# Norms between the stages of an eight-stage fp32 network, done one tile of 128 tokens at a time instead of for all 256 tokens at once

## The chip, the cores and the metric

One Trainium2 chip, of which this kernel uses one core. The metric is the device time of one execution in microseconds (us); lower is better. The core's engines run side by side, each through its own instruction stream: TensorE (PE, with its weight loads PEld), VectorE (DVE), ScalarE (ACT), GpSimd (POOL), and SyncE (SP), which issues most transfers. They wait for each other through semaphores.

## The reference

256 tokens of 1024 features pass through two blocks of four stages each. All is fp32.

```python
# block 1, RMSNorm BEFORE each stage; x keeps the plain sum
x = x + short_conv_mixer(rmsnorm(x, norm_mixer[0]))      # CONV
x = x + swiglu(rmsnorm(x, norm_ffn[0]))                  # FFN0, d_ff 2816
x = x + swa_sink_attention(rmsnorm(x, norm_mixer[1]))    # SWA
x = x + swiglu(rmsnorm(x, norm_ffn[1]))                  # FFN1
# block 2, LayerNorm AFTER each stage, x is replaced by it
x = layer_norm(1.414 * x + attention_mixer(x))           # NA
x = layer_norm(1.414 * x + squared_relu_mlp(x))          # MLP0, d_ff 4096
x = layer_norm(1.414 * x + mamba2_bidir_mixer(x))        # SSM
x = layer_norm(1.414 * x + squared_relu_mlp(x))          # MLP1 -> out
```

A norm needs the whole row of a token, so a token's norm can't begin before the last column of the stage ahead is summed into that token.

## The kernel before

**Chunks.** The weights come in 202 chunks of 128x2048 fp32 (1 MB), in one order for the whole kernel, through three slots. SyncE loads a chunk into `raw`; ACT rounds it to fp32r in `whi` (`hi(c)`, L828); DVE takes the rest, `raw - whi`, into `wlo` (`lo(c)`, L1185). `hi(c)` waits until TensorE is through with chunk `c - 3`. Every product is done in three matmuls: high by high, high by low, low by high. Activations are split the same way into `acthi` and `actlo`.

**Two shapes of product.** A *feature chunk* (`feature_chunk` L418; used for gate/up, MLP up, the convolution's and most of SSM's inputs) has a 128x128 block of the weights stationary and all 256 tokens of `acthi`/`actlo` moving: 8 contraction blocks x 3 x 2 feature halves = 48 matmuls of 256 columns, both token tiles in each. A *token chunk* (`token_chunk` L430; attention inputs, and the out-projections in `project` L454) has a 128-token tile stationary and 256 weight columns moving: 48 matmuls too, 24 for each tile `m`. A *down chunk* (`down_products` L487, the last one `last_down` L500 with L496) has a hidden tile stationary and 512 columns moving, 24 matmuls, 12 for each token tile. Its four results stand in the PSUM banks `ACC` to `ACC + 3`, kept open over a whole FFN or MLP by eight matmuls on zeros (`open_accumulators`, L477).

**The boundary between two stages.** There are seven boundaries where activations are made anew, called norm 1 (CONV to FFN0) to norm 7 (SSM to MLP1); norm 4 (FFN1 to NA) has no norm, only the split. The last norm, norm 8, leads to the output. At each of 1 to 7, in this order:

1. DVE adds the last pieces into `x` (L1195, or L1191 with the factor 1.414 followed by a `bn_stats`, L1193). For RMSNorm ACT squares each piece with a running sum (L836).
2. DVE sums the statistics of both tiles (L1201 or L1211); POOL makes 1/sqrt of them (`rsqrt`, L1671 and L1673); DVE scales both tiles, 128x1024 each (L1204 or L1215).
3. TensorE, which has filled its time with 24 matmuls on zeros (`keep_warm(24)`, L395), transposes 16 blocks of 128x128 into the `ACC` banks (`turn_acts`, L450).
4. ACT and DVE bring them into `acthi` and `actlo`, for norms 1 to 3 with the gain as a per-partition column (L846, L1223), for 5 to 7 after a pass with gain and bias (L856, L866, L1236, L1243). DVE also does one `lo(c)` in between. TensorE starts the first chunk two contraction blocks at a time as they come.
5. For norms 5 to 7 DVE then applies gain and bias to `x` itself, 4 passes of 128x1024 (`ln_finish`, L1252, L1254).

The stage before a boundary ends in four out-projection chunks (norms 1, 3, 5, 7) or in a last down chunk (norms 2, 4, 6, 8). Between FFN1 and NA TensorE also turns the relative position bias over (`flip_rpb`, L623: 16 matmuls of 512 columns, DVE adds the rest at L1454).

In each engine the order is that of the program text: an instruction that waits holds up all behind it on its engine.

## Time and profile before

| | |
|---|---|
| time, 3 runs | 1456.77 us median (1455.8 to 1458.49) |
| the profiled execution | 1455.31 us, of which 1453.5 us are the traced span |
| PE busy | 1359.7 us, 94% of the span |
| DVE busy | 922.3 us, 63% |
| ACT busy | 694.6 us, 48% |
| POOL busy | 210.1 us, 14% |
| TensorE's granted clock, mean | 0.96 |
| chain that ended last | PE 78%, DVE 16%, issue 2%, ACT 2% |

"Busy" of PE includes matmuls on zeros and slow ones. The granted clock is a share of 2.4 GHz: 1.00 is the upper level, 0.50 (1.2 GHz) the lower one, and a value between is a stretch with both. The busy time of a matmul in the rows is longer than the distance to the next one, since they overlap; the distance between starts is what a long series costs.

### The profile page before, as it was taken

To read this page: it belongs to the slowest core of one execution; us is meant where nothing else is said; L and a number is where in the kernel's file an instruction comes from. 1 tells how busy PE (TensorE), PEld (TensorE's weight loads), DVE (VectorE), ACT (ScalarE), POOL (GpSimd) and SP (SyncE) were. 2 spreads that over 40 slices of the span, in tenths; PEclk is the share of its full clock that TensorE was granted. 3 is DMA by queue.
4 is the path that set the end of the run, shared out by engine and by line. 5 is a ranking of instruction groups with operands and counts; after the bars stand their busy time and mean duration, and the time that the engine had idled before them with its cause. 6 is when DMAs were issued, how large, how long until landed. Compare 5 with 4: busy or idle time off the path is not lost.

```text
span 1453.5 us, 22749 instructions
## 1 busy us (share of the span) xinstructions
PE 1359.7 (94%) x9654; PEld 1274.9 (88%) x9654; DVE 922.3 (63%) x1036; ACT 694.6 (48%) x938; POOL 210.1 (14%) x227
## 2 busy tenths in 40 slices
PE   8999999998999999998999999988888878999997
PEld 8999999988899999797899999888787868899996
DVE  5655544557654454556775555787988997755555
ACT  5344444356544444335634444466656664344441
POOL 0000000016150000000000000012555665000000
PEclk9999999998799999998999999999999889999999
DMA  9554666543177656353046555544233214365552
GB/s 303 174 175 148 193 188 196 174 144 118 30 181 210 189 174 194 125 176 116 26 149 201 177 176 201 174 140 122 87 118 115 87 59 129 134 202 195 182 177 85
DMA packets 220324, 223.24 MB, mean 154 GB/s; under 512 B 7232, under 2 KB 204224, under 8 KB 220096
## 3 DMA queue, kind: packets, MB, share of 16 engines
q1 hardware_dynamic: 217472, 213.94, 46.7%
q10 hardware_dynamic: 1728, 5.76, 1.2%
q0 software_dynamic: 1024, 2.10, 0.8%
q8 instruction: 76, 1.25, 0.4%
q14 instruction: 24, 0.20, 0.0%
HBM read 220.72 MB, written 1.05 MB: 153 GB/s over the span
## 4 chain that ended last, share of the span: by engine, by line
PE 78%; DVE 16%; issue 2%; ACT 2%; POOL 1%; DMA 1%; POOLq 0%; DVEq 0%; SPq 0%; ACTq 0%
PE ps L487 19%; PE ps L402 13%; PE ps L403 13%; PE ps L404 13%; DVE ssm_taps L1544 4%; PE ps L413 4%; PE ps L415 4%; PE ps L414 4%; PE ps L749 3%; DVE wlo L1185 2%; DVE weight L1567 2%; PE ps L496 1%; PE ps L582 1%; DVE small L1374 1%; DVE weight L1573 1%
## 5 line engine op out<-in xcount | busy, mean ns | idle before, releaser
L1185 DVE TENSOR_TENSOR wlo<-raw,whi 128x2048 fp32r<-128x2048 f32 x202 | 470.3, 2329 | 228.3 <-ACT whi L828 228.3
L402 PE MATMUL ps<-acthi,whi 128*128 128x256 f32 x1664 | 477.7, 287 | 12.9 <-DVE actlo L1223 4.9
L403 PE MATMUL ps<-actlo,whi 128*128 128x256 f32 x1664 | 475.3, 286 | 0.0
L404 PE MATMUL ps<-acthi,wlo 128*128 128x256 f32 x1664 | 474.9, 285 | 0.0
L828 ACT ACTIVATE whi<-raw 128x2048 fp32r<-128x2048 f32 x202 | 385.1, 1907 | 143.5 <-PE ps L487 98.9
L402 PEld LDWEIGHTS ps<-acthi,whi 128*128 128x128 f32 x1664 | 324.1, 195 | 16.5 <-issue 11.4
L403 PEld LDWEIGHTS ps<-actlo,whi 128*128 128x128 f32 x1664 | 324.2, 195 | 2.5
L404 PEld LDWEIGHTS ps<-acthi,wlo 128*128 128x128 f32 x1664 | 323.8, 195 | 0.0
L1671 POOL TENSOR_SCALAR small<-small 128x2 f32<-128x2 f32 (+2 forms) x17 | 9.0, 528 | 1087.5 <-DVE small L1211 717.7
L487 PE MATMUL ps<-whi,hidhi 128*128 128x512 f32 x400 | 123.9, 391 | 0.0
L487 PE MATMUL ps<-wlo,hidhi 128*128 128x512 f32 x400 | 123.6, 390 | 0.0
L487 PE MATMUL ps<-whi,hidlo 128*128 128x512 f32 x400 | 123.4, 390 | 0.0
L413 PE MATMUL ps<-whi,acthi 128*128 128x256 f32 x368 | 106.7, 290 | 3.7 <-DVE actlo L1230 2.5
L414 PE MATMUL ps<-wlo,acthi 128*128 128x256 f32 x368 | 106.4, 289 | 0.0
L415 PE MATMUL ps<-whi,actlo 128*128 128x256 f32 x368 | 106.0, 288 | 0.0
L487 PEld LDWEIGHTS ps<-wlo,hidhi 128*128 128x128 f32 x400 | 75.1, 188 | 16.1
L487 PEld LDWEIGHTS ps<-whi,hidlo 128*128 128x128 f32 x400 | 75.1, 188 | 16.0
L1544 DVE SCALAR_TENSOR_TENSOR ssm_taps<-ssm_window,params,ssm_taps 128x256 f32<-128x256 f32 x128 | 73.1, 612 | 22.8 <-ACT ssm_taps L1026 21.1
L1693 POOL TENSOR_TENSOR cum<-table,ssm_small 128x512 fp32r<-128x512 f32 x64 | 74.6, 1194 | 60.0 <-PE ps L705 41.1
L902 ACT ACTIVATE gate_sb<-ps 128x256 f32<-128x256 f32 x44 | 16.9, 384 | 138.2 <-PE ps L404 138.2
L487 PEld LDWEIGHTS ps<-whi,hidhi 128*128 128x128 f32 x400 | 71.9, 189 | 11.9
L413 PEld LDWEIGHTS ps<-whi,acthi 128*128 128x128 f32 x368 | 73.1, 199 | 4.5 <-issue 4.1
(227 smaller groups left out, 1945.6 us busy)
## 6 DMA issues: line engine op xcount, KB each, us to landing
raw<-in_mlp_w SPq DMA_DIRECT2D x128, 512.0 KB, 4.3
raw<-in_ffn_w_gate_up SPq DMA_DIRECT2D x88, 512.0 KB, 5.2
raw<-in_ssm_w_in SPq DMA_DIRECT2D x50, 512.0 KB, 4.8
raw<-in_ffn_w_down SPq DMA_DIRECT2D x44, 512.0 KB, 4.3
raw<-in_conv_w_in SPq DMA_DIRECT2D x24, 512.0 KB, 5.7
raw<-in_attn_w_in SPq DMA_DIRECT2D x18, 512.0 KB, 4.5
raw<-in_ssm_w_out SPq DMA_DIRECT2D x16, 512.0 KB, 4.2
raw<-in_attn_w_qkv SPq DMA_DIRECT2D x12, 512.0 KB, 4.5
```

The lines of the kernel that those rows point to most:

```text
L402: e.matmul(out, hi[:, k, cols], acthi[:, k, :], start=k == 0 and f == 0, stop=False, skip_group_check=True)
L403: e.matmul(out, hi[:, k, cols], actlo[:, k, :], start=False, stop=False, skip_group_check=True)
L404: last = e.matmul(out, lo[:, k, cols], acthi[:, k, :], start=False, stop=k == KT - 1, skip_group_check=True)
L413: e.matmul(out, xh, hi[:, k, :], start=k == 0 and m == tokens[0], stop=False, skip_group_check=True)
L414: e.matmul(out, xh, lo[:, k, :], start=False, stop=False, skip_group_check=True)
L415: last = e.matmul(out, xl, hi[:, k, :], start=False, stop=k == KT - 1, skip_group_check=True)
L487: last = e.matmul(ps[:, ACC + 2 * m + n, :], p_, w_[:, k, n * 512:(n + 1) * 512], start=False, stop=False, skip_group_check=True)
L749: last = e.matmul(ps[:, OUT_BANKS[n], m * T:(m + 1) * T], p_, w_[:, k, :], start=half == m == k == q == 0, stop=half == 1 and k == KT - 1 ...
L828: e.activation(whi[s][:, :], raw[s][:, :], ACT.Copy).then_inc(*rounded.up(c))
L1185: e.tensor_tensor(wlo[s][:, :], raw[s][:, :], f32(whi[s][:, :]), ALU.subtract).then_inc(*split.up(c))
L1544: last = e.scalar_tensor_tensor(out=taps[:, q, f, :], in0=window[:, q, f, t:t + T], scalar=w, in1=taps[:, q, f, :], op0=ALU.mult, op1=ALU.add)
L1693: last = e.tensor_tensor(cum[d][k][:, :, :], spread(mask, [0, 4], [1, P]), spread(head_cols(v, m, d, g), [1, 4], [0, P]), ALU.mult)
```

## The change

**The tail of a stage.** The last two chunks do tile 0 first, then tile 1. Out-projection: chunk 2 tile 0, chunk 3 tile 0, chunk 2 tile 1, *transposes of tile 0*, chunk 3 tile 1. Down: both chunks' tile 0 (four groups of six matmuls), the earlier chunk's tile 1, then tile 1 of the last chunk in two halves, with the transposes of tile 0 before the first half (norms 2, 4) or between the halves (norm 6).

**The head of the next stage.** `first_feature_chunks` and `first_token_chunks` do two chunks together: chunk c tile 0, transposes of tile 1, chunk c+1 tile 0, chunk c tile 1, chunk c+1 tile 1. In a feature chunk a tile means 128 moving columns in place of 256, so its 48 matmuls become 96. At norm 6 the first chunk is the half chunk of SSM (24 matmuls, now 48).

**The norm.** It runs for a tile at a time, in halves of 512 columns. RMSNorm multiplies by scale and gain in one instruction (row gains come by a broadcast transfer into `lnrow`, also for norms 1 to 3); LayerNorm makes two such instructions a half, `(x - mean) * gain`, then `* rstd + bias`, and `x` is then final. POOL makes 1/sqrt once per tile. The split copies 128x512 at a time, two per tile. `keep_warm` at the boundaries, `open_accumulators`, `ln_finish` and the gain passes are gone. DVE's `lo` of the stage's second chunk stands between the adds and the scaling of tile 1.

**Others.** `flip_rpb` is done in two parts after the products of NA's chunks 3 and 5. The out-projection takes four PSUM banks at once: in CONV it waits for `conv_gated(3)` before its first matmul. The output leaves in four transfers in place of two.

TensorE's part first, then DVE's (`scale`, its LayerNorm branch, and `next_stage`):

```diff
-            def turn_acts(n, src, ready):
-                if n != 4:
-                    keep_warm(24)
...
+            def turn_tile(n, m):
+                src = h if n in (1, 2, 3) else x
+                for j in range(2):
+                    if n == 4:
+                        e.wait_ge(*added("ffn1", m, j))
+                    else:
+                        e.wait_ge(*scaled(n, m, j))
+                    for k in range(4):
+                        last = e.transpose(turn_bank(m, j)[:, k * P:(k + 1) * P], src[:, m, (4 * j + k) * P:(4 * j + k + 1) * P], ident)
+                    last.then_inc(*turned.up(n, m, j))
+            def feature_tile_products(s, m, fs, opens):
+                hi, lo = w8(whi[s]), w8(wlo[s])
+                for f in fs:
+                    out, cols = ps[:, s, f * T + m * P:f * T + (m + 1) * P], slice(f * P, (f + 1) * P)
+                    for k in range(KT):
+                        xh, xl = (v[:, k, m * P:(m + 1) * P] for v in (acthi, actlo))
+                        e.matmul(out, hi[:, k, cols], xh, start=k == 0 and opens, stop=False, skip_group_check=True)
+                        e.matmul(out, hi[:, k, cols], xl, start=False, stop=False, skip_group_check=True)
+                        last = e.matmul(out, lo[:, k, cols], xh, start=False, stop=k == KT - 1, skip_group_check=True)
+                    opens = False
+                return last
+            def first_feature_chunks(n, c, fs=(0, 1)):
+                s, s2 = c % SLOTS, (c + 1) % SLOTS
+                take(s)
+                e.wait_ge(*split(c))
+                e.wait_ge(*act_lo(n, 0, 1))
+                feature_tile_products(s, 0, fs, True)
+                turn_tile(n, 1)
+                take(s2)
+                e.wait_ge(*split(c + 1))
+                feature_tile_products(s2, 0, (0, 1), True)
+                e.wait_ge(*act_lo(n, 1, 1))
+                feature_tile_products(s, 1, fs, False).then_inc(*multiplied.up(c))
+                feature_tile_products(s2, 1, (0, 1), False).then_inc(*multiplied.up(c + 1))
...
+            def last_downs(st, before, hs_before, c, hs, hidden, n_norm):
+                for n in range(2):
+                    down_tile(before % SLOTS, hs_before, 0, n)
+                e.wait_ge(*split(c))
+                e.wait_ge(*hidden)
+                for n in range(2):
+                    down_tile(c % SLOTS, hs, 0, n).then_inc(*part.up(st, 0, n))
+                for n in range(2):
+                    last = down_tile(before % SLOTS, hs_before, 1, n)
+                last.then_inc(*multiplied.up(before))
+                if n_norm in (2, 4):
+                    turn_tile(n_norm, 0)
+                down_tile(c % SLOTS, hs, 1, 0).then_inc(*part.up(st, 1, 0))
+                if n_norm == 6:
+                    turn_tile(n_norm, 0)
+                down_tile(c % SLOTS, hs, 1, 1).then_inc(*multiplied.up(c))
...
             def project(st, c0, n_norm, piece_ready):
                for n in range(D // WIDE):
...
-                    take(s)
+                    if n == 0:
+                        for b in range(4):
+                            take(b)
...
+            def scale(n, m):
...
+                    e.bn_aggr(mean_var[n][:, 2 * m:2 * m + 2], stats[st][:, m * width:(m + 1) * width]).then_inc(*summed.up(n, m))
...
+                    for j in range(2):
+                        v = x[:, m, 512 * j:512 * j + 512]
+                        e.scalar_tensor_tensor(out=v, in0=v, scalar=mean_var[n][:, 2 * m:2 * m + 1],
+                                               in1=lnrow[:, 0, 512 * j:512 * j + 512], op0=ALU.subtract,
+                                               op1=ALU.mult).then_inc(*centred.up(n, m, j))
+                        e.wait_ge(*centred(n, m, j))
+                        if j == 0:
+                            e.wait_ge(*rms_made(n, m))
+                        e.scalar_tensor_tensor(out=v, in0=v, scalar=r, in1=lnrow[:, 1, 512 * j:512 * j + 512],
+                                               op0=ALU.mult, op1=ALU.add).then_inc(*scaled.up(n, m, j))
...
+            def next_stage(n, c, sum_tile):
+                sum_tile(0)
+                if n != 4:
+                    scale(n, 0)
                 if n < 8:
...
+                    make_acts(n, 0)
+                sum_tile(1)
+                if n < 8:
+                    lo(c)
+                if n != 4:
+                    scale(n, 1)
+                if n < 8:
+                    make_acts(n, 1)
```

## Rows read from the trace of the kernel before

**Rows 1.** Windows: length; busy (x count) of PE, PEld, DVE, ACT, POOL; PEclk, DMA.

```profile
296.31:301.75 5.44, 5.44 (x25) 4.50 (x24) 2.23 (x4) 3.80 (x6) 0.00 (x0) 1.00 0.58 193
301.75:309.24 7.49, 5.23 (x41) 4.61 (x40) 5.40 (x8) 3.50 (x11) 1.14 (x3) 1.00 0.00 1
...
606.22:617.45 11.23, 8.77 (x33) 4.68 (x32) 8.54 (x8) 3.73 (x5) 0.00 (x0) 0.99 0.00 0
617.45:623.21 5.76, 5.76 (x37) 5.76 (x38) 3.85 (x4) 0.12 (x1) 0.00 (x0) 0.73 0.68 203
741.16:749.05 7.89, 5.21 (x43) 4.62 (x41) 6.53 (x11) 3.18 (x7) 0.91 (x2) 1.00 0.28 87
749.05:754.81 5.76, 5.76 (x36) 5.76 (x36) 5.73 (x8) 2.87 (x3) 0.00 (x0) 0.70 0.43 160
931.06:939.40 8.34, 5.22 (x42) 4.62 (x40) 7.21 (x12) 3.18 (x7) 0.89 (x2) 1.00 0.37 113
939.40:944.36 4.96, 4.50 (x24) 4.29 (x25) 4.93 (x8) 2.88 (x3) 0.96 (x1) 0.70 0.60 200
1252.12:1260.76 8.64, 5.21 (x42) 4.61 (x41) 7.28 (x13) 3.18 (x7) 0.89 (x2) 1.00 0.14 44
```

**Rows 2.** Timeline, PE, norm 3: start, us, instructions, idle before and releaser.

```profile
411.06 0.28 PE L413 MATMUL ps<-whi,mixhi 128*128 128x256 f32 x1
411.18 0.28 PE L414 MATMUL ps<-wlo,mixhi 128*128 128x256 f32 x1
...
415.37 1.86 PE L450 MATMUL ps<-table,h 128*128 128x128 f32 x15 [0.33 <-DVE h L1204]
418.45 0.35 PE L402 MATMUL ps<-acthi,whi 128*128 128x256 f32 x1 [1.22 <-DVE actlo L1223]
```

**Rows 3.** Timeline, PE: attention scores in fp32r with 128 moving columns, both clocks.

```profile
348.49 0.27 PE L559 MATMUL ps<-k_lo,q_hi 64*128 64x128 f32 x1
348.60 0.27 PE L559 MATMUL ps<-k_hi,q_lo 64*128 64x128 f32 x1
...
352.39 0.41 PE L559 MATMUL ps<-k_hi,q_hi 64*128 64x128 f32 x1
352.60 0.41 PE L559 MATMUL ps<-k_lo,q_hi 64*128 64x128 f32 x1
```

**Rows 4.** Timeline, norm 2: 1/sqrt on POOL, then the first scaling.

```profile
303.68 0.19 POOL L1671 TENSOR_SCALAR small<-small 128x2 f32<-128x2 f32 x1 [194.28 <-DVE small L1201]
303.95 0.69 POOL L1673 TENSOR_TENSOR small<-small 128x2 f32<-128x2 f32 x1
...
304.69 0.77 DVE L1204 TENSOR_SCALAR h<-x,small 128x1024 f32<-128x1024 f32 x1 [1.09 <-POOL small L1673]
```

**Rows 5.** Timeline, norm 8: DVE and POOL after the last product.

```profile
1444.61 2.48 DVE L1659 SCALAR_TENSOR_TENSOR x<-x,small,lnrow 128x1024 f32<-128x1024 f32 x2
1444.72 1.23 POOL L1671 TENSOR_SCALAR small<-small 128x2 f32<-128x2 f32 x1 [189.38 <-DVE small L1211]
1446.03 1.62 POOL L1673 TENSOR_TENSOR small<-small 128x2 f32<-128x2 f32 x1
1447.75 2.48 DVE L1665 SCALAR_TENSOR_TENSOR x<-x,small,lnrow 128x1024 f32<-128x1024 f32 x2 [0.66 <-POOL small L1673]
```

**Rows 6.** Lines by form: busy us, mean ns, idle before.

```profile
L1185 DVE TENSOR_TENSOR wlo<-raw,whi 128x2048 fp32r<-128x2048 f32 x202 | 470.3, 2329 | 228.3 <-ACT whi L828 228.3
...
L1191 DVE SCALAR_TENSOR_TENSOR x<-x,ps 128x512 f32<-128x512 f32 x8 | 5.5, 687 | 4.8 <-PE ps L496 4.8
...
L1230 DVE TENSOR_TENSOR actlo<-ps,acthi 128x512 fp32r<-128x512 f32 x4 | 2.5, 682 | 0.0
```

**Rows 7.** Timeline, DVE, in front of norm 6.

```profile
924.18 2.29 DVE L1185 TENSOR_TENSOR wlo<-raw,whi 128x2048 fp32r<-128x2048 f32 x1 [1.12 <-ACT whi L828]
```

**Rows 8.** Timeline, PE: first half of the bias turning, ahead of NA.

```profile
606.22 3.59 PE L623 MATMUL ps<-bias,table 128*128 128x512 f32 x8
```

**Rows 9.** Timeline, DVE: CONV's last gating, after its last input chunk.

```profile
84.12 0.69 DVE L1292 TENSOR_TENSOR conv_y<-ps,conv_y 128x512 f32<-128x512 f32 x1 [0.56 <-PE ps L404]
```

More of the change, by code:

```diff
@@ L455, in project @@
+            def project(st, c0, n_norm, piece_ready):
                 for n in range(D // WIDE):
@@ L645, in na @@
                 free.clear()
-                project("na", NA + 9, lambda p: out_lo("na", 4 + p))
+                project("na", NA + 9, 5, lambda p: out_lo("na", 4 + p))
             def ssm():
                 s = SSM % SLOTS
-                take(s)
-                e.wait_ge(*split(SSM))
-                hi, lo = (w8(w)[:, :, P:2 * P] for w in (whi[s], wlo[s]))
-                for p in range(4):
-                    e.wait_ge(*act_lo(6, p))
-                    for k in (2 * p, 2 * p + 1):
-                        for q, (w_, a_) in enumerate(((hi, acthi), (hi, actlo), (lo, acthi))):
-                            last = e.matmul(ps[:, s, 0:T], w_[:, k, :], a_[:, k, :], start=k == q == 0,
-                                            stop=k == KT - 1 and q == 2, skip_group_check=True)
-                last.then_inc(*multiplied.up(SSM))
                 def turn_dt():
@@ L736, in turn_y, with out_products @@
                         last.then_inc(*y_turned.up(half, k))
+                def out_products(half, n, m):
+                    c = ssm_out(half, n)
+                    hi, lo = (w8(w[c % SLOTS]) for w in (whi, wlo))
+                    hi_part, lo_part = ((acthi, actlo), (mixhi, mixlo))[half]
+                    opens = half == 0 and (m == 0 if n < 2 else n == 2)
+                    for k in range(KT):
+                        xh, xl = (v[:, k, m * P:(m + 1) * P] for v in (hi_part, lo_part))
+                        for q, (p_, w_) in enumerate(((xh, hi), (xh, lo), (xl, hi))):
+                            last = e.matmul(out_place(n, m), p_, w_[:, k, :], start=opens and k == q == 0,
+                                            stop=half == 1 and k == KT - 1 and q == 2, skip_group_check=True)
+                    return last
                 def out_chunk(half, n):
@@ new lines, in make_acts, with next_stage @@
+            def make_acts(n, m):
+                for j in range(2):
+                    e.wait_ge(*turned(n, m, j))
+                    e.activation(acthi[:, 4 * j:4 * j + 4, m * P:(m + 1) * P],
+                                 turn_bank(m, j).rearrange("p (k n) -> p k n", k=4), ACT.Copy).then_inc(*act_hi.up(n, m, j))
+            def next_stage(n, st, c, pieces):
+                for piece in pieces:
+                    square(st, 0, piece)
+                make_acts(n, 0)
+                hi(c)
+                for piece in pieces:
+                    square(st, 1, piece)
+                make_acts(n, 1)
@@ L906, in ffn @@
                         hi(ffn_down(c0, t - 1) + 2)
-                hi(c0 + 34)
-                for m in range(MT):
-                    for n in range(2):
-                        square(st, m, n)
+                next_stage(2 if st == "ffn0" else 4, st, c0 + 34, (0, 1))
             def mlp(st, c0):
@@ L1206, in ln_scale, with input_norm @@
-            def ln_scale(n):
-                st = NORM_OF[n]
-                width = 6 * PIECES[st]
-                for m in range(MT):
+            def input_norm():
+                e.wait_ge(*rms_made(0))
+                for m in range(MT):
+                    e.tensor_scalar(h[:, m, :], x[:, m, :], rms[0][:, m:m + 1], None, ALU.mult).then_inc(*scaled.up(0, m))
+                lo(0)
+                for b in range(4):
+                    e.wait_ge(*act_hi(0, 2 * b + 1))
+                    for k in (2 * b, 2 * b + 1):
+                        last = e.scalar_tensor_tensor(
+                            out=actlo[:, k, :], in0=bank2(ACC + b)[:, k % 2, :], scalar=column("norm_mixer0", k),
+                            in1=f32(acthi[:, k, :]), op0=ALU.mult, op1=ALU.subtract)
+                    last.then_inc(*act_lo.up(0, b))
@@ new lines, in scale @@
+            def scale(n, m):
+                st = NORM_OF[n]
+                r = rms[n][:, m:m + 1]
+                if n < 4:
+                    e.wait_ge(*squared(st, m, PIECES[st] - 1))
+                    e.tensor_reduce(mean_square[n][:, m:m + 1], stats[st][:, m * PIECES[st]:(m + 1) * PIECES[st]], AX,
+                                    ALU.add).then_inc(*summed.up(n, m))
+                    if m == 0:
+                        e.wait_ge(rows_landed[n], 16)
+                    e.wait_ge(*rms_made(n, m))
+                    for j in range(2):
+                        cols = slice(512 * j, 512 * j + 512)
+                        e.scalar_tensor_tensor(out=h[:, m, cols], in0=x[:, m, cols], scalar=r, in1=lnrow[:, 0, cols],
+                                               op0=ALU.mult, op1=ALU.mult).then_inc(*scaled.up(n, m, j))
+                else:
+                    width = 6 * PIECES[st]
```

577 lines of the change are left out of this document (261 added, 316 removed).

## The prediction

> **What bounds the kernel now.** I read the page first: PE is busy 94% of the span and holds 78% of the chain that ended last, DVE 16%. So a microsecond counts when TensorE has more to do or has to wait; the other engines matter where TensorE waits for them. Then the windows of the boundaries, because the change touches little else. The reader is to see three things in them [rows 1]. Norm 2 takes 7.49 us from the last product of the stage before to the first of the next, norms 5, 6 and 7 take 7.89, 8.34 and 8.64 us, and norm 4 takes 11.23 us with the bias turning inside. PE looks busy in most of that, but only because of 24 matmuls on zeros. And after norms 4 to 7 the clock falls: 0.73, 0.70 and 0.70 in the windows that follow. Norm 3 runs from 411.42 (two steps after the last row of 411.18 starts its own) to 418.45, 7.03 us [rows 2]; norm 1 is built in the same way and taken as equal. Together some 58 us are up for gain, of which the transposes stay. Last I read the timeline of TensorE for the distance between starts, since this change makes more matmuls of half the width.
>
> **The price of a narrow matmul.** With 256 moving columns the distance is 0.12 us [rows 2], so a feature chunk is 48 x 0.12 = 5.76 us. No matmul of the exact new form (128 rows, 128x128 stationary in fp32r, 128 moving) is in the trace. Its nearest relations are the score products in fp32r with 128 moving columns: 0.11 us at the full clock, 0.21 at the low one [rows 3]; and the transposes, 128 columns over all 128 rows, 15 of them in 1.86 us, or about 0.114 after taking off the length of the last [rows 2]. Both load a new 128-column stationary tile for each matmul, as the new ones do. Half the columns thus save a twelfth of the time, not half: what is left is the weight load. From below, if time went by moving columns alone, it would be 0.06. I take 0.11, because both rows have it, at two clocks. Per norm with two full feature chunks (1, 3, 5, 7): 4 x 48 x 0.11 - 2 x 48 x 0.12 = 21.1 - 11.5 = **+9.6 us**. Norm 6, a half chunk and a full one: 144 x 0.11 - 72 x 0.12 = **+7.2**. Norms 2 and 4 lead to token chunks, where the matmuls are only reordered: 0.
>
> The Trainium skill (TensorE: Matmul & The Clock Gate, Back-to-back issue gap) says that a stream of load and matmul pairs settles at about 81 ns a matmul for 128 columns. By that the extra would be 4.0 us a full boundary, not 9.6. Its LDWEIGHTS section gives columns / 1.2, 107 ns for 128 columns, and there the trace agrees: 0.11 us [rows 3].
>
> **What tile order leaves of the waits.** I follow both tiles with these durations: piece add 0.69 on 512 columns, `bn_stats` alike, split copy 0.68, `lo` 2.29 [rows 6, 7]; 1/sqrt on POOL 1.01 from its start to the scaling [rows 4]; a scaling in two-input form 2.48/4 = 0.62 a half [rows 5]. Time zero is the start of the last two chunks' tile 0.
>
> - *Norms 1, 3.* Chunk 3 tile 0 is done at 5.76; DVE's add and ACT's square of 0.4 each, then 1/sqrt, give the first half at 9.0. TensorE is free at 8.64 (three half chunks of 2.88): it waits 0.35, then 0.25 for the other half. Transposes of tile 1 come after a 5.28 us half pair and wait for nothing. Idle 0.6.
> - *Norms 5, 7.* LayerNorm adds `bn_stats`, and its `(x - mean) * gain` runs on DVE while POOL makes 1/sqrt. At norm 8 such an overlap is in the trace: POOL's two instructions take 1.23 and 1.62 us, against 0.19 and 0.69 at norm 2, and the first ends as DVE's first pass does [rows 4, 5]. A pass of half the length costs some 0.6 of that at each tile. Norm 5: waits 0.7 + 0.85 at tile 0, 0.55 + 0.85 at tile 1, idle 2.95. Norm 7: both pieces of tile 0 wait for one signal, and tile 1's adds do too: 1.5 + 0.85 + 1.35 + 0.85 = 4.55.
> - *Norm 2.* Tile 0 of the last down chunk is done 4.1 us in, but DVE is in a `lo` until 5.6 (norm 6's row: it ends at 926.47, 6.3 us after the tail begins [rows 7]). TensorE is free for the transposes at 8.2 and waits 1.7 + 0.25. Tile 1: `lo` (2.3) stands ahead of its scaling, and a token half chunk covers only 2.88: wait 2.3 + 0.25. Idle 4.5.
> - *Norm 6.* Hidden part 0.2; tile 0: 1.9 + 0.9, then 0.1 for the split; tile 1: the half chunk covers 2.64 us only, and DVE has two adds, two `bn_stats`, `lo` and LayerNorm ahead, 7 us: wait 4.8 + 0.85. Idle 8.75.
> - *Norm 4.* No norm; idle 0.
>
> **The sum for each boundary** is narrow extra + transposes 1.83 + idle - old gap - 0.96 for the eight opening matmuls (8 x 0.12; FFN and MLP only) - what the old low clock lost. At 0.70 the window after norm 5 has 36 matmuls where 48 fit: with the tail of it 1.56 us; after norm 4, 37: 1.3; SSM's first 24 matmuls took 4.96 for 2.88, with its successor's start 2.4 [rows 1].
>
> - norms 1 and 3: 9.6 + 1.83 + 0.6 - 7.03 - 0.96 = +4.0 each
> - norm 2: 1.83 + 4.5 - 7.49 = -1.2
> - norm 4: 1.83 + 6.9 (16 turning matmuls at (3.59 - 0.59)/7 = 0.43 [rows 8], now in NA) - 11.23 - 1.3 = -3.8
> - norm 5: 9.6 + 1.83 + 2.95 - 7.89 - 0.96 - 1.56 = +4.0
> - norm 6: 7.2 + 1.83 + 8.75 - 8.34 - 2.4 = +7.0
> - norm 7: 9.6 + 1.83 + 4.55 - 8.64 - 0.96 - 1.56 = +4.8
>
> Besides: CONV's out-projection began under the last gating; it now waits until that is done. The gating takes 0.69 us and starts some 0.2 after the last input product, and the release adds a little [rows 9]: +1.05. The output: tile 0 leaves early and tile 1 is done in halves, but tile 0's LayerNorm (POOL slowed) pushes tile 1's adds back; DVE ends about 1 us earlier than the old 1450.2 [rows 5], and transfers of half the size end sooner: -1.2 (0 to -2.5). The row loads for the gains (0.5 MB three times) lie beside 47% busy transfers: 0. `ln_finish` is DVE work beside TensorE: 0, and at SSM the chain behind the first chunk begins only when that chunk is done, so 0 there too. Sum: +18.7 us.
>
> The new clock: PE's idle at norms 4 to 6, by window length less busy time, was 2.46, 2.68 and 3.12 us, and the low level followed; it takes up 21 to 24 of the next 48 steps' time [rows 1]. Norm 6 now idles 4.8 us in one piece: the next some 27 narrow matmuls would cost 0.21 in place of 0.11, +2.8. Norms 2 and 7 idle 2.3 and 2.35 about one set of transposes: an even chance each of 1.4 to 1.6, +1.5. In all **+23 us** on the profiled execution's 1455.31, so 1478.3; the median of the runs is 1.5 above that execution: **1479 us**.
>
> **Rivals.**
> - *Narrow matmuls cost by their columns*, 0.06 us. Then 45.6 us of extra fall away, and the shorter cover gives back some 2.3 us at norms 1, 3, 5 and 7 and 1.3 at norm 6, since tile 1's norm is no longer hidden: 1479 - 45.6 + 10.5 = 1444. Against it: 0.11 in both relations [rows 2, 3]. This one ends on the other side; the border is at a price where 192 x (0.11 - p) x 4 + 144 x (0.11 - p) less the returned waits is 23 us, p about 0.08.
> - *A price between*, 0.08. 27 us fall away, some 4 return: 1456, no difference. The skill's 81 ns stands for this one.
> - *The tile chain is longer than I made it*: ACT's `hi`, POOL under DVE's passes, and a clock that falls at norms 2, 5, 6 and 7 alike and stays low for the whole pair (narrow matmuls at 0.21 rather than 0.11 cost 5 us more for every 5 us of work): 1486 to 1494.
> - *The boundaries hide fully*, narrow price as forecast but no idle and no low clock: 1479 - 26 (21.95 idle, 4.3 clock) = 1453. Only if DVE did tile 1 before its `lo`, which the order forbids; a small chance.
>
> **How the numbers follow.** Forecast 0.65 (its own range 1468 to 1486), longer chain 0.19, between 0.06, by columns 0.07, fully hidden 0.03. 0.2%, 2.9 us, is about what a measurement of this kernel can tell from no change. Faster: 0.07; same: 0.03 + 0.03 = 0.06 with part of the middle case; slower: the rest, 0.87. The range 1463 to 1490 leaves out the cases below and the worst of the long chain.
>
> **What would show it.** Right: the feature matmuls of 256 columns fewer by 456 in all, twice as many of 128 at 0.11 between starts, each full pair of chunks 21 us; no L395 after the start; waits of the transposes for DVE's scaling, longest at norm 6 tile 1, nearly none at norms 1 and 3; POOL's 1/sqrt over 1.5 us at norms 5 to 8; NA's chunks 3 and 5 with 3.4 us of turning each. Wrong: a distance of 0.06 to 0.08, or pairs at a low clock beyond norm 6, or waits for `wlo` behind the pair (each slot is freed a whole pair late; I found 1 us and more to spare).

## The result, and the profile after

| | before | after |
|---|---|---|
| time, 4 runs each | 1457.55 us median (1455.8 to 1458.49) | 1494.47 us median (1493.23 to 1495.04) |
| the profiled execution's span | 1453.5 us | 1493.2 us |
| PE busy | 1359.7 us, 94% | 1394.3 us, 93% |
| TensorE's granted clock, mean | 0.960 | 0.957 |

The ratio is 1.0253, 95% interval 1.0239 to 1.0268: slower by 37 us. The forecast was 1479 us and the range ended at 1490, so the sign was right and the size was not. The lines of the page that carry this (busy time and share by engine; the clock in 40 slices; the chain that ended last; groups of instructions with busy time, mean ns of one, and idle time before them):

```profile
PE 1394.3 (93%) x9934; PEld 1307.5 (88%) x9934; DVE 920.9 (62%) x1031; ACT 686.2 (46%) x914; POOL 219.3 (15%) x241
...
PEclk9999999998899999999999999779989889999999
...
PE 70%; DVE 11%; POOL 9%; issue 8%; ACT 2%; DMA 1%; SPq 0%; POOLq 0%; DVEq 0%; ACTq 0%
...
L414 PE MATMUL ps<-acthi,whi 128*128 128x256 f32 x1520 | 436.5, 287 | 5.5 <-DVE wlo L1266 2.9
...
L426 PE MATMUL ps<-acthi,whi 128*128 128x128 f32 x304 | 89.4, 294 | 2.4 <-DVE x L1272 1.8
```

PE has 35 us more busy time, almost the whole loss, so this is work or a slow clock and not idle time. The narrow matmuls stand in three groups of 304, 912 in all, in place of 456 wide ones. Their mean of 294 ns is *longer* than that of the wide ones, 287, which their work can't explain: it is pulled up by some that ran at half the clock. The row PEclk shows where to look. Its two slices of 7 are numbers 25 and 26, counted from 0, or 933 to 1008 us, which begins with norm 6. The same row of the kernel before has 9 in both places:

```profile
PEclk9999999998799999998999999999999889999999
```

The shares of the chain that ended last have moved as well (POOL from 1% to 9%, issue from 2% to 8%), but they don't say where time was lost: SSM, where most of POOL's part lies, grew by 1.6 us only, as the table below shows. The windows of the boundaries show more (length; busy time and count of each engine; granted clock; DMA):

```profile
120.00:134.28 14.28, 14.28 (x131) 14.28 (x130) 5.18 (x4) 4.79 (x5) 0.00 (x0) 1.00 0.35 105
431.55:443.42 11.87, 11.87 (x108) 11.87 (x108) 3.69 (x4) 2.61 (x3) 11.87 (x21) 1.00 1.01 198
...
759.16:775.27 16.11, 16.11 (x148) 16.11 (x145) 6.07 (x6) 5.55 (x5) 0.00 (x0) 1.00 0.36 131
912.00:940.90 28.90, 28.75 (x172) 25.44 (x171) 17.05 (x14) 11.85 (x10) 0.00 (x0) 1.00 0.52 164
940.90:957.00 16.10, 9.07 (x54) 7.11 (x53) 13.11 (x19) 3.60 (x4) 2.60 (x4) 0.92 0.37 120
957.00:982.65 25.65, 25.65 (x123) 25.65 (x121) 5.54 (x4) 4.59 (x4) 0.96 (x1) 0.50 0.27 82
1284.70:1299.20 14.50, 11.82 (x87) 11.18 (x88) 9.89 (x15) 3.60 (x4) 1.31 (x2) 0.88 0.21 73
1299.24:1315.35 16.11, 16.11 (x147) 16.11 (x146) 6.07 (x6) 5.55 (x5) 0.00 (x0) 1.00 0.43 131
```

The last 144 narrow matmuls of norms 5 and 7 take 16.11 us at a clock of 1.00, or 0.112 us each. The last 120 of norm 6 (957.00 to 982.65) take 25.65 us at 0.50, 0.214 each. TensorE is busy all through that window; nothing interrupts it, and the clock doesn't rise before its end. What came before it is on PE's timeline:

```profile
943.99 0.66 PE L484 MATMUL ps<-table,x 128*128 128x128 f32 x4 [1.46 <-DVE x L1321]
945.44 0.66 PE L484 MATMUL ps<-table,x 128*128 128x128 f32 x4 [0.80 <-DVE x L1321]
...
949.30 0.27 PE L426 MATMUL ps<-acthi,whi 128*128 128x128 f32 x1
949.41 0.28 PE L427 MATMUL ps<-actlo,whi 128*128 128x128 f32 x1
...
954.79 1.12 PE L484 MATMUL ps<-table,x 128*128 128x128 f32 x4 [4.33 <-DVE x L1321]
956.24 1.11 PE L484 MATMUL ps<-table,x 128*128 128x128 f32 x4 [0.33 <-DVE x L1321]
957.01 0.46 PE L426 MATMUL ps<-acthi,whi 128*128 128x128 f32 x1
957.26 0.41 PE L427 MATMUL ps<-actlo,whi 128*128 128x128 f32 x1
```

The brackets give the idle time before a row and what ended it. At 949 the narrow matmuls start 0.11 apart. Then TensorE waits 4.33 us for DVE's scaling of tile 1 (L1321), four transposes that took 0.66 take 1.12, and the narrow matmuls now start 0.21 apart. The wait was forecast as 4.8; the 120 slow matmuls were not.

To see where the 39.7 us between the spans lie, I measured each stretch in both traces from landmark to landmark and set the forecast beside it. A norm's stretch runs from the start of the last two chunks' tile 0 to the end of the next stage's first two chunks; norm 4's holds all of NA up to norm 5's, since the bias is turned there.

| stretch | measured | forecast |
|---|---|---|
| start to end of CONV's inputs | +1.6 | 0 |
| CONV out-projection's wait for banks | +1.1 | +1.05 |
| norm 1 | +5.1 | +4.0 |
| norm 2 | -1.8 | -1.2 + 0.75 |
| inside SWA | +2.4 | 0 |
| norm 3 | +4.1 | +4.0 |
| norm 4 and NA, with the bias turning | -4.9 | -3.8 |
| norm 5 | +4.6 | +4.0 |
| **norm 6** | **+20.1** | +7.0 + 2.8 |
| inside SSM | +1.6 | 0 |
| norm 7 | +6.6 | +4.8 + 0.75 |
| MLP1 and the output | -0.8 | -1.2 |
| sum | +39.7 | +23 |

Norm 6 alone has 10.3 of the missing 16.7.

### The profile page after: what moved, and what is told of

It is laid out like the page before. It is cut to its first block, busy times and chain, and to the rows that moved or that the text cites. A ratio compares the mean times of both kernels' runs of the same rounds, so it can differ in the third digit from the quotient of the medians.

```text
span 1493.2 us, 23309 instructions
## 1 busy us (share of the span) xinstructions
PE 1394.3 (93%) x9934; PEld 1307.5 (88%) x9934; DVE 920.9 (62%) x1031; ACT 686.2 (46%) x914; POOL 219.3 (15%) x241
## 3 DMA queue, kind: packets, MB, share of 16 engines
HBM read 222.25 MB, written 1.05 MB: 150 GB/s over the span
## 4 chain that ended last, share of the span: by engine, by line
PE 70%; DVE 11%; POOL 9%; issue 8%; ACT 2%; DMA 1%; SPq 0%; POOLq 0%; DVEq 0%; ACTq 0%
PE ps L585 17%; PE ps L414 10%; PE ps L416 10%; PE ps L415 10%; POOL cum L1768 3%; PE ps L828 3%; DVE wlo L1266 2%; PE ps L437 2%; PE ps L439 2%; PE ps L438 2%; PE ps L428 2%; PE ps L427 2%; PE ps L426 2%; POOL xdec L1777 1%; POOL small L1747 1%
## 5 line engine op out<-in xcount | busy, mean ns | idle before, releaser
L414 PE MATMUL ps<-acthi,whi 128*128 128x256 f32 x1520 | 436.5, 287 | 5.5 <-DVE wlo L1266 2.9
L415 PE MATMUL ps<-actlo,whi 128*128 128x256 f32 x1520 | 434.5, 286 | 0.0
L416 PE MATMUL ps<-acthi,wlo 128*128 128x256 f32 x1520 | 434.2, 286 | 0.0
L414 PEld LDWEIGHTS ps<-acthi,whi 128*128 128x128 f32 x1520 | 296.6, 195 | 8.3 <-issue 3.1
L415 PEld LDWEIGHTS ps<-actlo,whi 128*128 128x128 f32 x1520 | 296.2, 195 | 2.4
L416 PEld LDWEIGHTS ps<-acthi,wlo 128*128 128x128 f32 x1520 | 296.1, 195 | 0.0
L1745 POOL TENSOR_SCALAR small<-small 128x1 f32<-128x1 f32 (+3 forms) x24 | 13.7, 572 | 1105.8 <-DVE small L1309 726.6
L426 PE MATMUL ps<-acthi,whi 128*128 128x128 f32 x304 | 89.4, 294 | 2.4 <-DVE x L1272 1.8
L428 PE MATMUL ps<-acthi,wlo 128*128 128x128 f32 x304 | 89.1, 293 | 0.0
L427 PE MATMUL ps<-actlo,whi 128*128 128x128 f32 x304 | 89.1, 293 | 0.0
```

The costliest lines, as they stand in the source:

```text
L414: e.matmul(out, hi[:, k, cols], acthi[:, k, :], start=k == 0 and f == fs[0], stop=False, skip_group_check=True)
L415: e.matmul(out, hi[:, k, cols], actlo[:, k, :], start=False, stop=False, skip_group_check=True)
L416: last = e.matmul(out, lo[:, k, cols], acthi[:, k, :], start=False, stop=k == KT - 1, skip_group_check=True)
L426: e.matmul(out, hi[:, k, cols], xh, start=k == 0 and opens, stop=False, skip_group_check=True)
L427: e.matmul(out, hi[:, k, cols], xl, start=False, stop=False, skip_group_check=True)
```

## The experiments

Two theories for norm 6. **A:** a stream of 128-column matmuls can hold TensorE's upper level but can't bring it back; 256-column ones bring it back. **B:** once fallen, the clock stays down for its own time, some 25 us, whatever runs. Beside them stood the price of a narrow matmul: the stationary load or the moving columns.

### 1. Work in the 4.3 us wait

```diff
                 feature_tile_products(s, 0, fs, True)
+                if n == 6:
+                    keep_warm(32)
                 turn_tile(n, 1)
```

> At norm 6 only, 32 matmuls on zeros (256 columns) are put in front of the transposes of tile 1, into the 4.33 us in which TensorE waits there. Theory A (the low clock came from that idle, and a stream of 128-column matmuls keeps it low): the clock stays at 1.00 over the pair, its 120 narrow matmuls go from 0.214 to 0.112 us each, 25.6 to 13.4 us; the kernel is 12 us faster, some 1482. Rival B (the low clock there has to do with the narrow matmuls alone, or with this place in the kernel): the pair stays at 0.214 and the time at 1494.

Measured: 1480.53 us (1478.03 to 1483.78), 1.0163 times before, interval 1.0143 to 1.0182. The changed kernel stood at 1.0253, so 32 matmuls on zeros take back 0.9%, 13 us. PE's timeline, then the window of the last 120 narrow matmuls:

```profile
950.05 4.05 PE L407 MATMUL ps<-zero 128*128 128x256 f32 x32
954.54 0.66 PE L484 MATMUL ps<-table,x 128*128 128x128 f32 x4 [0.44 <-DVE x L1323]
955.99 0.66 PE L484 MATMUL ps<-table,x 128*128 128x128 f32 x4 [0.79 <-DVE x L1323]
```

```profile
956.40:969.83 13.43, 13.43 (x123) 13.43 (x122) 5.43 (x4) 4.58 (x4) 0.97 (x1) 1.00 0.27 85
```

The transposes start at the same moment as without the zeros (954.54 and 954.79): they cost nothing. The same 120 matmuls take 13.43 us in place of 25.65. So the low level cost 12.2 us there, and the wait was its trigger.

### 2. Zeros in the middle of the slow stretch

```diff
                 e.wait_ge(*act_lo(n, 1, 1))
+                if n == 6:
+                    keep_warm(48)
                 feature_tile_products(s, 1, fs, False).then_inc(*multiplied.up(c))
```

> At norm 6 only, 48 matmuls on zeros (256 columns) are put in the middle of the slow pair, after the 48 narrow matmuls of the second chunk's tile 0. Theory A: the clock goes up during or right after them, as it does under wide matmuls after norms 4 to 7 of the kernel before, and the 72 narrow matmuls that are left take 0.112 us each, 8.1 us in place of 15.4; the 48 zeros cost 7 to 10 us, so the time stays within 3 us of 1494. Rival B (the level is held down for a fixed time of some 25 us after the idle): the 72 go on at 0.214 and the time is 10 us longer, 1504.

One run, 1494.16 us. Windows: 48 narrow matmuls, the 48 wide ones on zeros, the last 72 narrow ones.

```profile
955.60:965.93 10.33, 10.33 (x51) 10.33 (x49) 3.29 (x3) 2.40 (x2) 0.96 (x1) 0.50 0.33 104
965.93:973.81 7.88, 7.88 (x49) 7.88 (x50) 0.00 (x0) 0.00 (x0) 0.00 (x0) 0.70 0.00 0
973.81:981.80 7.99, 7.99 (x74) 7.99 (x73) 2.29 (x1) 2.19 (x2) 0.00 (x0) 1.00 0.00 0
```

The clock is 0.50 under the narrow ones, rises under the wide ones, and is 1.00 under the narrow ones behind them, at 0.111 each. It is up by 973.8. In this run it was at 0.50 from 950.2 to 970.7, 20.5 us, which is less than B's 25; kernel 5 below, with 10.2 us at the same place, shows more clearly that there is no fixed time of 25 us. Under wide matmuls the clock came back and under the narrow ones here it had not, as A says; how far A holds elsewhere, kernels 4 and 5 show. The 48 zeros cost 7.88 us and give back about as much, hence the equal time.

### 3 and 4. What a narrow matmul is paid for

Here blocks 1 to 6 of the eight contraction blocks are cut at every narrow chunk: in the third kernel they move 64 columns in place of 128, in the fourth they have 64 stationary columns. Each leaves out half of those blocks' products.

```diff
+                        w = P if k in (0, KT - 1) else P // 2
-                        e.matmul(out, hi[:, k, cols], xh, start=k == 0 and opens, stop=False, skip_group_check=True)
+                        e.matmul(out[:, 0:w], hi[:, k, cols], xh[:, 0:w], start=k == 0 and opens, stop=False, skip_group_check=True)
...
```

```diff
+                        w = P if k in (0, KT - 1) else P // 2
+                        half = slice(f * P, f * P + w)
-                        e.matmul(out, hi[:, k, cols], xh, start=k == 0 and opens, stop=False, skip_group_check=True)
+                        e.matmul(out[0:w, :], hi[:, k, half], xh, start=k == 0 and opens, stop=False, skip_group_check=True)
...
```

> In the first feature chunks, contraction blocks 1 to 6 of 8 move 64 columns in place of 128 (the other half of those products is left out). If the stationary load sets the price, the distance stays at 0.112 us and the time within 2 us of 1494. If moving columns set it, 684 matmuls save some 0.05 us each, 34 us, to 1460.

> In the first feature chunks, contraction blocks 1 to 6 of 8 have 64 stationary columns in place of 128 and still move 128 tokens (half of those products is left out). If the stationary load sets the price, their distance falls from 0.112 to about 0.06 us and the time by 684 x 0.05 = 34 us and more at the slow pair, to 1455 to 1460. If moving columns set it, no change, 1494.

Third kernel, one run: **1570.4 us**, 76 more than the change, where no theory had a large loss. Its PE timeline and two windows, all at norm 1:

```profile
115.33 0.28 PE L427 MATMUL ps<-acthi,whi 128*128 128x64 f32 x1
115.44 0.28 PE L428 MATMUL ps<-actlo,whi 128*128 128x64 f32 x1
...
117.15 1.93 PE L485 MATMUL ps<-table,h 128*128 128x128 f32 x8
118.73 0.46 PE L427 MATMUL ps<-acthi,whi 128*128 128x128 f32 x1
```

```profile
112.00:116.50 4.50, 4.50 (x43) 4.50 (x42) 3.25 (x4) 0.12 (x2) 0.74 (x2) 1.00 0.32 108
118.70:149.50 30.80, 30.80 (x147) 30.80 (x145) 6.82 (x6) 6.45 (x7) 0.00 (x0) 0.50 0.29 83
```

With half the columns moved, matmuls still start 0.11 apart. That is the answer asked for: between 128 and 64, the moving columns don't set the price. The 76 us are something else. After a first chunk of this stream the clock is at 0.50 without any idle time inside it (ahead of it TensorE had waited 0.21 and 0.52 us, as in the changed kernel, whose clock stayed up there), and it stays there to the end of the pair. The same happened at norms 3, 5 and 7 (at norm 3 with a single wait of 0.23 us in the 8 us before); at norm 6 the clock fell in the 4.33 us wait, as in the changed kernel. Each time it stayed low to the end of the pair, and was back 2.2 to 5.1 us after the first wide matmul behind it.

Fourth kernel, one run: 1456.68 us, 38 less than the change. PE's timeline at norm 1, behind its first three full matmuls:

```profile
112.54 0.22 PE L428 MATMUL ps<-acthi,whi 128*64 128x128 f32 x1
112.60 0.22 PE L429 MATMUL ps<-actlo,whi 128*64 128x128 f32 x1
...
113.26 0.27 PE L428 MATMUL ps<-acthi,whi 128*128 128x128 f32 x1
113.37 0.28 PE L429 MATMUL ps<-actlo,whi 128*128 128x128 f32 x1
```

With 64 stationary columns the distance is 0.06; back at 128 it is 0.11. 684 such matmuls save 0.05 each, some 34 us. At norm 1, with the clock at 1.00 in both kernels, the pair's last 144 matmuls take 10.51 us (116.84 to 127.35) in place of 16.1. The stationary load sets the price of the narrow form. (The 38 us are not this alone: at norm 6 the higher clock adds to it, and longer waits take from it.) And at norm 6, after an idle stretch of 5.26 us, this stream brought the clock back:

```profile
939.78:950.04 10.26, 10.26 (x122) 10.26 (x121) 4.32 (x4) 4.59 (x4) 0.96 (x1) 0.84 0.33 100
```

So A has to be put more exactly. This stream of 128 moving columns was followed by the upper level; the streams held back to 0.21 by their loads, at norm 6 of the changed kernel and in kernel 3, were not. What in them makes the difference isn't shown, and the next kernel has an exception.

### 5. Wide products at norm 6 alone

In `first_feature_chunks`, at norm 6, tile 1 is turned first and then both chunks go in 256 columns:

```diff
+                if n == 6:
+                    take(s)
+                    e.wait_ge(*split(c))
+                    turn_tile(n, 1)
+                    for j in range(2):
+                        e.wait_ge(*act_lo(n, 1, j))
+                        last = feature_products(s, range(4 * j, 4 * j + 4), fs)
...
+                    feature_products(s2).then_inc(*multiplied.up(c + 1))
+                    return
```

> The changed kernel, with 256-column matmuls in the first two chunks at norm 6 only, after tile 1's activations; no zeros are put in, so TensorE idles there in one piece of 6 us and more and the clock falls. Theory A: under wide matmuls the clock comes back within some 6 us, as after norms 4 to 7 of the kernel before; the pair's 72 wide matmuls take some 11 us and the time is some 12 us below the change's 1494. Rival B (a fall there lasts 25 us whatever runs): the pair takes 15 us at 0.214 and the next chunk is slow too, 1490 or more.

One run, 1489.93 us. PE's longest wait, and the window of most of the 72 wide matmuls:

```profile
956.69 1.08 PE L484 MATMUL ps<-table,x 128*128 128x128 f32 x4 [7.39 <-DVE x L1333]
```

```profile
959.30:970.20 10.90, 10.90 (x77) 10.90 (x78) 5.28 (x3) 4.78 (x5) 0.97 (x1) 0.82 0.36 102
```

The idle time is 3 us longer than in the changed kernel, and the clock falls too, but under 256-column products it comes back: 0.82 in this window, where 120 narrow matmuls never left 0.50. It was at 0.50 for 10.2 us in all (953.0 to 963.2). A again, at this place.

Norm 6's stretch takes 35.5 us here and 50.3 in the changed kernel, so the change at norm 6 gained 14.8, more than the 12 expected. That the kernel gained only 4.5 has another reason, at the next boundary. From the first product of the out-projection before norm 7 to the last product of the kernel it takes 228.2 us (from 1250.66), the changed kernel 221.2 (from 1262.77), with the same code. At norm 7 the clock fell under the first narrow chunk:

```profile
1284.09:1292.39 8.30, 8.30 (x42) 8.30 (x41) 4.63 (x6) 0.00 (x0) 1.31 (x2) 0.50 0.37 126
1292.39:1294.30 1.91, 1.91 (x11) 1.91 (x11) 0.17 (x1) 0.60 (x1) 0.00 (x0) 0.50 0.03 9
1294.30:1310.25 15.95, 15.95 (x145) 15.95 (x144) 6.22 (x6) 5.55 (x5) 0.00 (x0) 1.00 0.40 133
```

Narrow matmuls 0.21 apart, then tile 1's eight transposes without a wait (1292.39), two more narrow ones, and the clock is at 1.00. No wide matmul stands in between. So the strict form of A, that only wide matmuls bring the clock back, is false: here it came back 10.2 us after its fall, under narrow matmuls and transposes; at norm 6 of the changed kernel it didn't within 25.65 us of narrow matmuls alone. Whether the transposes make that difference was not tested; in kernel 3 eight of them (117.15) did not bring it back. And the fall itself came in one execution and not in another of the same code, so a single run can be some 7 us off by this alone.

### 6. DVE's `lo` behind the scaling at norm 6

```diff
-                if n < 8:
+                if n < 8 and n != 6:
                     lo(c)
                 if n != 4:
                     scale(n, 1)
+                if n == 6:
+                    lo(c)
```

> The changed kernel, with DVE's lo of the second chunk behind the scaling of tile 1 at norm 6 only. If it is the lo (2.29 us) in front of the scaling that makes the 4.33 us wait long enough for the clock to fall, the wait is 2.0 us now, another of some 2 us comes for the split weights, and the clock stays up or falls late: 5 to 12 us faster than 1494. If the sum of the idle counts and not its longest piece, the clock falls as before and nothing changes.

One run, 1492.75 us. PE's waits, and the window of the last 120 narrow matmuls:

```profile
950.70 0.66 PE L484 MATMUL ps<-table,x 128*128 128x128 f32 x4 [2.26 <-DVE x L1321]
952.15 0.85 PE L484 MATMUL ps<-table,x 128*128 128x128 f32 x4 [0.79 <-DVE x L1321]
954.44 0.45 PE L426 MATMUL ps<-acthi,whi 128*128 128x128 f32 x1 [1.45 <-DVE wlo L1266]
```

```profile
954.44:980.07 25.63, 25.63 (x120) 25.63 (x121) 5.60 (x4) 3.17 (x3) 0.96 (x1) 0.50 0.40 123
```

The wait of 4.33 became 2.26, but `lo` is late now and adds 1.45. No piece is long, and the clock fell all the same, in the second group of transposes (0.66, then 0.85), so before the piece of 1.45. Making one wait shorter is no cure if the idle pieces stay close together; filling it was. Of the 1.7 us less than the change's time nearly all was there before norm 6 was reached: CONV's out-projection began at 84.88, against 86.64, by a clock that stayed at 1.00 at the start (more on this below). Norm 6's stretch is only 0.6 us shorter.

### 7. Tile order for the norms, wide products everywhere

```diff
                 take(s)
                 e.wait_ge(*split(c))
-                e.wait_ge(*act_lo(n, 0, 1))
-                feature_tile_products(s, 0, fs, True)
+                bank = TOP if n == 6 else ACC + 3
+                for _ in range(24):
+                    e.matmul(ps[:, bank, 0:T], zero[:, 0:P], zero[:, :], start=True, stop=True)
                 turn_tile(n, 1)
+                for j in range(2):
+                    e.wait_ge(*act_lo(n, 1, j))
+                    last = feature_products(s, range(4 * j, 4 * j + 4), fs)
...
-                feature_tile_products(s2, 0, (0, 1), True)
...
+                feature_products(s2).then_inc(*multiplied.up(c + 1))
```

Beside it DVE does `lo(c)` behind tile 1's split at these norms, and the out-projection takes its banks one by one again.

> Tails and norms by tile as in the change, but at norms 1, 3, 5, 6 and 7 the first two feature chunks are done in 256-column matmuls, once tile 1's activations are there too; 24 matmuls on zeros stand in the wait, DVE's lo comes after tile 1's split, and CONV's out-projection takes its banks one by one. Norms 2 and 4 stay as changed. Theory A (the loss is the 456 added weight loads at 0.112 us, and the low clock at norm 6; what tile order does to the waits is itself a gain): the gap from last to first product falls from 7.0 to some 5.1 us at norms 1 and 3 and from 7.9 to 8.6 to some 5.5 at 5, 6 and 7, with the clock at or near 1.00 after them; with norm 2's, norm 4's and norm 8's gain and the opening matmuls the kernel comes to 1430 to 1440, faster than both. Rival C (tile order itself lengthens the chains, two 1/sqrt and halves in place of whole passes): 1450 to 1460.

Measured: 1453.35 us (1449.41 to 1456.04, 11 runs), 0.9977 times before, interval 0.9967 to 0.9986. It beats both kernels, but by 3.4 us and not by the 17 to 27 expected. PE's timeline at norm 1:

```profile
110.46 3.13 PE L495 MATMUL ps<-zero 128*128 128x256 f32 x24 [0.52 <-DVE x L1280]
115.44 0.38 PE L414 MATMUL ps<-acthi,whi 128*128 128x256 f32 x1 [0.98 <-DVE actlo L1331]
```

The last product's step ends at 109.79, and the next stage's first product starts at 115.44: 5.65 us, of which 0.52 are a wait for the banks, against 7.03 [rows 2]. At norm 3, without that wait, it is 5.19. That is the gain I had counted; I had forgotten that tile 0's transposes, about 1.25 us, and a wait of 0.2 for them now stand inside the tail instead. What is left of it at norm 1 is next to nothing, so the 1.0 us gained there are the eight opening matmuls (0.96) that are gone. By landmarks against before: norms 1, 2, 3, 4, 5 and 7 give -1.0, -2.0, -1.5, -3.8, -1.8 and -1.1; norm 6 costs 2.9 (four waits, 4.5 us in all, and a clock of 0.83 under its 72 wide products, 937.02 to 947.26), SWA 2.3, SSM 3.0, the start 1.5. The time is in rival C's range, but not for its reason: at six of the seven boundaries tile order was the shorter one.

### 8. The same with more zeros

26 zeros in place of 24 (44 at norm 6) and ahead of the wait for the banks, 12 before norm 6's first transposes, 28 in place of 24 at the input, and in SSM's out-projection each bank is free when its own tile is added.

```diff
+                bank, zeros = (TOP, 44) if n == 6 else (ACC + 3, 26)
+                for _ in range(zeros):
+                    e.matmul(ps[:, bank, 0:T], zero[:, 0:P], zero[:, :], start=True, stop=True)
                 turn_tile(n, 1)
+                take(s)
+                e.wait_ge(*split(c))
...
                 if n_norm == 6:
+                    keep_warm(12)
                     turn_tile(n_norm, 0)
...
-                    free[n] = added("ssm", 1, 3)
+                    free[n] = added("ssm", n % 2, 3)
```

> The version with wide heads, its zeros moved ahead of the wait for a free bank, 44 of them and 12 more in front of tile 0's transposes at norm 6, 28 in place of 24 at the input, and SSM's banks released by the tile that sits in them. Theory A says that clock levels, not work, hold the version before it back: at its norm 6 the pair took 10.24 us for 8.64 and the tail's last six products 2.5 for 1.4, and at the input the clock fell once (1.6 us). With it at 1.00 in both places 4 to 6 us go, to some 1448. Rival C (norm 6 is bound by DVE's two LayerNorm passes per tile): the pair is quick but starts as late, and only 2 to 3 us go.

Measured: 1454.14 us (1447.96 to 1455.37, 12 runs), 0.9981 times before, interval 0.9971 to 0.9990; no different from the seventh. Windows: the start, norm 6, and SSM soon after it.

```profile
14.00:40.00 26.00, 25.33 (x211) 25.36 (x212) 18.42 (x22) 12.81 (x10) 0.00 (x0) 1.00 0.92 284
934.00:943.99 9.99, 9.39 (x76) 9.01 (x75) 7.66 (x5) 4.59 (x4) 0.98 (x1) 1.00 0.49 154
960.00:968.00 8.00, 8.00 (x47) 8.00 (x48) 7.31 (x10) 5.28 (x6) 1.85 (x2) 0.66 0.43 131
```

What it aimed at it got: the clock is 1.00 at the start and at norm 6. (That the 28 zeros did it at the start isn't shown: kernel 9 has them too, and 0.93 there.) Then the stages behind give part of it back: inside SSM 48 wide matmuls behind a wait of 4.03 us take 8.26 us at 0.66 (from 959.92), where the seventh kernel has the same wait and 7.30 at 0.77 (from 963.19). Why, by the earlier arrival or otherwise, is open.

### 9. Norm 2's first chunk finished before the second

```diff
                 turn_tile(n, 1)
+                if n == 2:
+                    e.wait_ge(*act_lo(n, 1, 1))
+                    token_products(s, acthi, actlo, bank_of(s), 1, opens=False).then_inc(*multiplied.up(c))
                 take(s2)
...
```

The changed kernel otherwise, and 28 zeros at the input.

> The changed kernel with norm 2's first chunk finished for both tiles before the second one is begun, and 28 zeros in place of 24 at the input. If the 2.3 us that SWA lost are the head norms, which DVE begins when the first chunk is whole and repeats five times in 5.6 us each, the head transposes' wait of 2.0 us goes, and TensorE waits some 2.5 us longer for tile 1 at norm 2: about even. At the input, if the 1.6 us lost there are a clock fall set off by 0.3 us more idle, the clock stays at 1.00 and the out-projection of CONV starts 1.6 us earlier. Time 1491 to 1495. If neither, the landmarks stay.

One run, 1494.11 us. PE's timeline before SWA's head transposes in the changed kernel:

```profile
352.14 2.84 PE L627 MATMUL ps<-table,qkv 128*128 128x128 f32 x24 [2.04 <-DVE qkv L1512]
```

and here, with the first product after tile 1's transposes at norm 2 and the windows of that chunk and of the start:

```profile
319.66 0.58 PE L437 MATMUL ps<-whi,acthi 128*128 128x256 f32 x1 [1.41 <-DVE actlo L1331]
...
355.01 2.81 PE L631 MATMUL ps<-table,qkv 128*128 128x128 f32 x24 [0.78 <-ACT qkv L1066]
```

```profile
319.66:332.00 12.34, 12.34 (x81) 12.34 (x82) 5.74 (x5) 4.79 (x6) 1.88 (x2) 0.76 0.25 86
```

```profile
14.00:40.00 26.00, 25.29 (x198) 25.32 (x199) 18.46 (x22) 11.32 (x10) 0.00 (x0) 0.93 0.88 282
```

The wait in SWA is back to 0.78, and the one behind it, before the first scores, from 0.87 to 0.13, both as in the kernel before. So they do come from the pair. But without the second chunk's tile 0 as cover TensorE waits 1.41 us for tile 1's split, and the clock drops to 0.76 behind that. By norm 3's first transposes this kernel is 1.3 us later than the changed one (418.43 against 417.15), so it lost more than it got back. The start stays at 0.93.

## Why the prediction was right in sign and wrong in size

**The price of a narrow matmul: right.** Forecast 0.11, measured 0.112 over 144 in a row, and shown to be the stationary load's (kernels 3 and 4). The rivals by columns (0.06) and between (0.08) fall. The Trainium skill's figure of about 81 ns for a stream of load and matmul pairs (TensorE: Matmul & The Clock Gate, Back-to-back issue gap) isn't borne out for this fp32r stream. By the Trainium skill's formula for a weight load (TensorE: Matmul & The Clock Gate, LDWEIGHTS), columns / 1.2, one of 128 columns takes an estimated 107 ns. The measured 0.112 us is near that.

**The waits: right in the main.** Each boundary but norm 6 came within 1.4 us, and CONV's wait for banks within 0.1. Norm 6's wait was 4.33 for 4.8. The even chance of a low clock came true at norm 7 (0.88 in 1284.70 to 1299.20) and not at norm 2 (1.00 in 318.20 to 326.80).

**The failed step: the clock at norm 6.** "Norm 6 now idles 4.8 us in one piece: the next some 27 narrow matmuls would cost 0.21 in place of 0.11, +2.8." The fall came as forecast. The 27 was carried over from the windows after norms 4 to 6, where the low level was said to take up 21 to 24 steps' time [rows 1]. (That was itself a loose reading: after norm 4 of the kernel before, the trace has 14 matmuls 0.21 apart, from 617.45 to 620.36, and the next ones 0.12 apart.) But those matmuls were 256 columns wide. Under narrow ones the low level did not end: 120 x (0.214 - 0.112) = 12.2 us, not 2.8. This is 9.4 of norm 6's 10.3 missing us and shown by kernels 1 and 2. The term with its measured size would have moved the forecast to some 1488. (The sum's last step is also 0.8 short: 1478.3 and 1.5 are 1479.8, not 1479.)

The Trainium skill (TensorE: Matmul & The Clock Gate, Part 1 on the clock gate) calls the warm-up a span of time and not a number of matmuls, whatever is issued in it. The window of 25.65 us with TensorE busy throughout and the clock at 0.50 says otherwise.

**The rival "tile chain is longer"** (0.19, 1486 to 1494) had the right consequence, a whole pair at the low clock, by the wrong cause. The chain was not longer, and only norm 6 fell for the whole pair. That the measured time lies next to its range is luck.

**Terms that were missing**, together some 8 us:
- *SWA, +2.4.* I put the first pair's effect on the chain behind it at nothing. At norm 2 the pair makes its first chunk whole only 2.9 us before the second. DVE, ACT and POOL work through the chunks one by one (head norm), and that series started later: DVE's first reduction at 325.51 with the pair ending at 326.8, against 316.56 and 320.8. Kernel 9, where both waits go back, 2.0 us together, shows the cause of all but 0.4 us.
- *The banks of the first chunk.* It opens in a bank that DVE has to empty by the add of tile 1: waits of 0.52, 0.51 and 1.29 us at norms 1, 5 and 7, none at norm 3. Read from the timelines; not taken away by itself.
- *The start, +1.6.* The window 14 to 40 us has a clock of 0.93, before it had 1.00. This is not shown to be the change's doing: kernel 6 is the changed kernel in all that comes before norm 6, and its clock held 1.00 there. What goes with it in the traces is the first wait, between the zeros and the first transpose. It is 0.41 us before, 0.03 in kernel 6 and 0.00 in kernel 8, which held 1.00, and 0.64 to 1.32 in the changed kernel and kernels 1 to 5, 7 and 9, where it fell. It differs from run to run with the time at which the first zeros end (9.05 in the changed kernel, 9.68 in kernel 6, with 24 zeros in each). Whether the wait is the cause wasn't tested.
- *SSM, +1.6.* The low level of norm 6 reached 2.55 us into it (982.65 to 985.20 at 0.50): the 96 matmuls behind the pair take 12.88 us, against 11.73 before. That is 1.15 of it; the rest is open.

**What it was offset by:** norm 2 and norm 4 gained 1.4 and 1.1 us more than forecast. At norm 2 the two waits were 1.26 and 1.88 us, where 4.5 were expected in all. Norm 4's 1.1 is probably chance: it lies in NA's attention, from the first head transposes to the out-projection, which took 46.37 us before, 45.37 in the changed kernel and 46.42 in the seventh, whose code is the same there, at a clock of 0.85, 0.92 and 0.85.

## What to carry to other kernels

When the stationary block changes with every matmul, the load sets the pace, and halving the moving columns doubles the number of matmuls for nearly no time saved each: here about 10 us for each pair of chunks, more than the idle time that it hid. An idle stretch of a few microseconds is priced by what comes *after* it: before a stream that is bound by its loads, fill the stretch with matmuls on zeros, or put wide matmuls behind it. And since the clock fell at the start and at norm 7 in some executions and not in others of the same code, read the clock of every stage before you credit an edit elsewhere with a few microseconds of a single run. And before removing filler work, look for the new place of the idle time, since it may be the filler's next home (32 zeros were worth 13 us).

## What the runs showed of the hardware that I had not expected

- A stream of fp32r matmuls with 128 loaded and 128 moved columns held the upper level (16.11 us at 1.00) but did not regain it in 25.65 us of unbroken work. 48 matmuls of 256 columns regained it in under 7.88 us. It isn't a matter of width alone: in kernel 5 the clock was back at 1.00 at 1294.3, 10.2 us after its fall, with 128-column matmuls and eight transposes only.
- With 64 moved columns the upper level was lost with no idle time in the stream (1.00 in 112 to 116.5, 0.50 in 118.7 to 149.5), at the pairs of norms 1, 3, 5 and 7; that kernel took 76 us longer than the change.
- The distance between such matmuls followed the loaded columns: 0.11 us for 128 whether 64 or 128 are moved, 0.06 for 64.
- Idle pieces of 2.26 and 0.79 us with four transposes between them (kernel 6) were followed by the low level just as one of 4.33 was.
